# VectorE's work ahead of attention in another order: clears while it waits, the latent's products first, the rotary key's rotation last

## The reference

```
h = rmsnorm(x, g_pre_mix)
q_sb, k_sb, v_sb, q_mla, ckv, k_rope, gate_a, gate_b = jnp.split(h @ w_in, SPLIT_POINTS, axis=-1)
...
q_nope, q_rope = q_mla[..., :MLA_NOPE], rope(q_mla[..., MLA_NOPE:], pos)
ckv = rmsnorm(ckv, ckv_gain)        # the latent, 128 wide
k_rope = rope(k_rope, pos)          # the rotary key: x1*cos - x2*sin, x1*sin + x2*cos
...
o_sb = sb_attend(q_sb, k_sb, v_sb, ...)             # stick-breaking attention, 8 heads of 64
o_lat = mla_attend(q_lat, q_rope, ckv, k_rope, ...) # latent attention
```

## Time and profile before

| | us |
|---|---|
| median of 3 runs | 1912.62 (1909.57 to 1912.67) |
| profiled execution | 1912.68 |
| its span, first to last instruction | 1910.9 |
| TensorE busy | 1853.4 (97%) |
| GpSimd busy | 987.1 (52%) |
| VectorE busy | 964.0 (50%) |
| ScalarE busy | 558.1 (29%) |

### The profile page before, as it was taken

How to read it: one execution, slowest core, us unless ns; L and a number is a source line. 1 busy time by engine, 2 the same in 40 slices (tenths; PEclk the granted TensorE clock), 3 DMA queues, 4 the chain that set the end, 5 groups by cost and what they waited for, 6 DMA issues and landing times. The chain is left out here.

```text
span 1910.9 us, 33493 instructions
## 1 busy us (share of the span) xinstructions
PE 1853.4 (97%) x14390; PEld 1786.2 (93%) x14390; DVE 964.0 (50%) x1536; ACT 558.1 (29%) x1164; POOL 987.1 (52%) x584
## 2 busy tenths in 40 slices
PE   8999999999999999999999899999999999999999
PEld 8888888999999999999998888889999999999998
DVE  6687665322655531524657756653327555225153
ACT  4344443212422221202344344431124222212021
POOL 6454414555455555556554534245555555555553
PEclk9999999999999999999999999999999999999999
DMA  5232211224122222222342212112242222222222
GB/s 173 95 101 67 73 35 49 89 89 147 67 89 89 89 89 89 89 82 86 103 144 85 95 57 72 39 56 92 86 148 73 86 87 88 88 89 89 81 88 92
DMA packets 74804, 168.37 MB, mean 88 GB/s; under 512 B 6112, under 2 KB 33632, under 8 KB 74656
## 3 DMA queue, kind: packets, MB, share of 16 engines
q1 hardware_dynamic: 67328, 158.69, 25.5%
q10 hardware_dynamic: 7328, 7.54, 1.2%
HBM read 156.41 MB, written 9.79 MB: 87 GB/s over the span
## 5 line engine op out<-in xcount | busy, mean ns | idle before, releaser
L1501 PE MATMUL ps<-xn,wsp 128*128 128x272 f32 x7872 | 1013.1, 289 | 21.4 <-issue 13.1
L1501 PEld LDWEIGHTS ps<-xn,wsp 128*128 128x128 f32 x7872 | 993.2, 189 | 27.8 <-issue 16.9
L583 POOL CAST wsp<-raw 128x1024 fp32r<-128x1024 f32 (+2 forms) x278 | 298.4, 1073 | 778.5 <-DMA raw<-in_wstream 626.7
L585 POOL TENSOR_TENSOR wsp<-raw,wsp 128x1024 fp32r<-128x1024 f32 (+2 forms) x278 | 665.3, 2393 | 22.3
L1501 PE MATMUL ps<-R,wsp 128*128 128x272 f32 x3840 | 486.3, 288 | 0.1
L1501 PEld LDWEIGHTS ps<-R,wsp 128*128 128x128 f32 x3840 | 482.7, 189 | 1.3 <-DVE xT L1074 0.5
L1045 DVE SCALAR_TENSOR_TENSOR R<-ps,R 64x256 fp32r<-64x256 f32 (+8 forms) x232 | 127.6, 560 | 72.6 <-ACT R L713 22.7
L1394 DVE TENSOR_TENSOR mix<-ps,rstd 128x272 f32<-128x272 f32 x88 | 38.8, 441 | 202.9 <-PE ps L1501 192.5
L936 ACT ACTIVATE mix<-vv 128x2 f32<-128x2 f32 x88 | 17.9, 204 | 363.0 <-DVE mix L1396 363.0
L1045 DVE SCALAR_TENSOR_TENSOR R<-mix,R 128x544 fp32r<-128x544 f32 (+1 forms) x82 | 74.5, 909 | 80.9 <-ACT R L957 66.9
L1402 DVE SCALAR_TENSOR_TENSOR ps<-mix,vv,ps 128x546 f32<-128x546 f32 x88 | 69.4, 788 | 55.6 <-ACT ps L945 55.6
(11 more groups left out here) (225 smaller groups left out, 1526.8 us busy)
## 6 DMA issues: line engine op xcount, KB each, us to landing
raw<-in_wstream SPq DMA_DIRECT2D x233, 512.0 KB, 3.7
raw<-in_wstream SPq DMA_DIRECT2D x48, 128.0 KB, 2.7
raw<-in_wstream SPq DMA_DIRECT2D x16, 384.0 KB, 3.1
raw<-in_kc SPq DMA_DIRECT2D x8, 512.0 KB, 4.1
raw<-in_vc SPq DMA_DIRECT2D x8, 512.0 KB, 4.2
xT<-in_x_in SPq DMA_DIRECT2D x8, 272.0 KB, 5.1
out_k_out<-mix ACTq DMA_DIRECT2D x8, 272.0 KB, 2.9
xT<-in_x_in SPq DMA_DIRECT2D x1, 2176.0 KB, 8.2
```

The costliest lines, as they stand in the source:

```text
L583: nc.gpsimd.tensor_copy(dst[:, 0, 0:w], part).then_inc(S["w_hi"], 1)
L585: nc.gpsimd.tensor_tensor(dst[:, 1, 0:w], part, dst[:, 0, 0:w].bitcast(F32), ALU.subtract).then_inc(S["w_lo"], 1)
L1501: mm = pe.matmul(z[:, h], w[:, x, (k0 + k) * P:(k0 + k + 1) * P], rhs[:, y, k, h * HT:(h + 1) * HT], start=(k == 0 and (x, y) == (0, 0)), ...
```

## The change

VectorE's list ahead of attention is reordered in both layers, and ScalarE's follows. The two clears come first (in layer 0 ahead of the wait for `roots`, in layer 1 behind the wait for `rstd_done`). Then come the two products with rstd, of the latent and of the rotary key; the four small copies; q's low parts; the latent's normalised product and its low part; k. The rotation of the rotary key and its low part come behind k and ahead of v. ScalarE stores and copies the rotary key behind k's copies. No instruction is added or removed, and TensorE's, GpSimd's and SyncE's lists are the same.

```diff
--- before.py
+++ after.py
@@ -847,11 +847,11 @@
                     rsqrt(("cn", 0), LORA)
                     nc.scalar.preload_act_table_set("sigmoid_and_others")
                     rt_tile()
-                    rope_parts(0)
                     act.wait_ge(S["dve_read"], dread(("cn", 0)))
                     act.dma_start(c_out[layer], craw).then_inc(S["c_st"], 16)
                     ac(cT[:, 0], craw, ACT.Copy).then_inc(S["c_hi"], 1)
                     qk_tile(("k", 0))
+                    rope_parts(0)
                     if layer > 0:
                         act.wait_ge(S["x_st"], 16)
                     else:
@@ -1058,15 +1058,12 @@
                             dve.wait_ge(S["acc_done"], n)
                             v.tensor_tensor(acc[:], acc[:], sq[j % 2], ALU.add).then_inc(S["acc_done"], 1)
 
+                    if layer > 0:
+                        dve.wait_ge(old["rstd_done"], 5)
+                    v.memset(q_smp.bitcast(F32), 0.0).then_inc(S["zeroed"], 1)
+                    v.memset(qr_smp.bitcast(F32), 0.0).then_inc(S["zeroed"], 1)
                     if layer == 0:
                         dve.wait_ge(pre["roots"], 1)
-                    else:
-                        dve.wait_ge(old["rstd_done"], 5)
-                    for a in range(QB):
-                        ins = v.tensor_copy(sq[1][:, DEC * a:DEC * (a + 1)], rstd[:, SEQ:T])
-                    ins.then_inc(S["rt_set"], 1)
-                    v.memset(q_smp.bitcast(F32), 0.0).then_inc(S["zeroed"], 1)
-                    v.memset(qr_smp.bitcast(F32), 0.0).then_inc(S["zeroed"], 1)
 
                     def times_rstd(dst, t):
 
@@ -1107,7 +1104,6 @@
 
                     def rope_rotate(n, t):
                         if n == 0:
-                            times_rstd(halves(rope[0]), t).then_inc(S["dve_read"], 1)
                             dve.wait_ge(S["dve_read"], dread(t))
                             dve.wait_ge(S["trig_in"], 16)
                         else:
@@ -1273,16 +1269,20 @@
 
 
                     times_rstd(halves(craw), ("c", 0)).then_inc(S["dve_read"], 1)
-                    rope_rotate(0, ("kr", 0))
+                    times_rstd(halves(rope[0]), ("kr", 0)).then_inc(S["dve_read"], 1)
+                    for a in range(QB):
+                        ins = v.tensor_copy(sq[1][:, DEC * a:DEC * (a + 1)], rstd[:, SEQ:T])
+                    ins.then_inc(S["rt_set"], 1)
                     qk_tile(("q", 0))
                     dve.wait_ge(S["rstd_done"], 1)
                     dve.wait_ge(S["c_sq"], 1)
                     v.scalar_tensor_tensor(halves(craw), halves(craw), vv[:, V_CG:V_CG + 1], ptile(("cn", 0)),
                                            ALU.mult, ALU.mult).then_inc(S["dve_read"], 1)
-                    rope_low(0)
                     dve.wait_ge(S["c_hi"], 1)
                     lo(cT[:, 1], craw, cT[:, 0], "c_lo")
                     qk_tile(("k", 0))
+                    rope_rotate(0, ("kr", 0))
+                    rope_low(0)
                     if layer > 0:
                         dve.wait_ge(S["x_st"], 16)
                     v_tile(("v", 0))
```

## The result

The change makes the kernel slower: 1922.81 us (median of 6 runs, 1920.41 to 1927.88) against 1911.78 us (6 runs of before, 1909.57 to 1913.07). The ratio is 1.0053, 95% interval 1.0037 to 1.0069. The forecast was 1926.1 with 1916 to 1930. The profiled execution took 1923.15 us with a span of 1921.4, 10.5 us more than before's.

A forecast was written before the change was run, and what follows sets the result against it. TensorE, busy 97% of the span, bounds the kernel, so only its waits count. Layer 0's loss of 1.6, layer 1's 7.6 and the clock's 4.2 add 13.4 us to 1912.68: 1926.1 us, range 1916 to 1930.

The forecast's parts named there:

- the wait of 7 to 8 us: Sign of a right forecast: TensorE waits this long for VectorE's product ahead of v's transposition (L1669) in layer 1.
- The place: Ahead of v's transposition TensorE waited only 0.21 and 0.28 us for VectorE's product of v, which has no slack.
- The gain of 3.54 us in layer 0: Layer 0's head: k starts 1.58 us earlier and v follows k without a wait, at 36.74 instead of 40.28.
- The stalls: v's transposition comes later behind the moved rotation: 1.6 us lost in layer 0, gain included, and 7.6 in layer 1.
- rival 1: Layer 1's low part gets in before GpSimd's subtraction: 5.3 us lost in place of 7.6, total 1923.8; chance 0.25.
- The low part is 0.14 us too late and waits for 999.13: Layer 1: rotary key's low part, ready at 996.88, misses GpSimd's subtraction start at 996.74 and waits for its end.
- the cheap branch: Layer 1: the low part gets in before GpSimd's subtraction, 5.3 us lost; chance 0.25.
- the dear branch: Layer 1: the low part is held by GpSimd's subtraction, 7.6 us lost; the forecast itself, chance 0.42.
- The hold by GpSimd: VectorE operations with two SBUF inputs wait for the running GpSimd operation and end 0.58 us after it.
- The rival of an undisturbed rotation: Rotation runs unheld in both layers: +0.45 us, TensorE waits some 2.5 and 1.9, clock unaffected, 1913.1 us; chance 0.13.
- The clock: TensorE's clock falls to half at each layer's stall ahead of v's transposition, costing 2.1 us each, 4.2 in sum.
- I carry the shift to the end undiminished: Behind v's product attention finds its inputs as before, so the whole +13.4 us reaches the end of the kernel.

The follow-up runs named there:

- the move alone: Kernel before, with only the rotation, low part and high part of the rotary key moved behind k; 1925.21 us, ratio 1.0062.
- its undoing in two ways: Two kernels against the changed one: rotation and its parts moved on behind v's product, 1910.47 us; or back to their places of before, 1909.03 us.
- layer 1 alone: New order in layer 1 only, layer 0 in the order of before; 1921.90 us, ratio 1.0045 to the kernel before.
- the busy wait: Changed kernel plus 36 extra matmuls between step 0's scores and v's transposition, in both layers; 1920.26 us, ratio 1.0048 to before.
- layer 0 alone: New order in layer 0 only, layer 1 in the order of before; 1914.46 us, ratio 1.0009 to the kernel before.

## Why the prediction was right

The mechanism came as I had it in both layers, and the time lies in the range. One term of the sum was too large: the wait of 7 to 8 us that I named as a sign for layer 1 was 5.57.

**The place.** v's product has no slack, and the rotation was put ahead of it: right in both layers, shown by the move alone and by its undoing in two ways.

**The gain of 3.54 us in layer 0.** Measured 3.45 us with the rotation in its old place (q's start to the transposition). The term was right, but the reason for its second half was not the only one: I put 1.96 us of it down to the rotation's leaving the way of the normalised product. The move alone shows that this does take away the wait ahead of v, but it is enough as well that everything in front starts earlier. So the part of the change that costs nothing brings the whole gain by itself.

**The stalls.** Layer 0: 1.6 us forecast, 2.19 - 0.47 = 1.72 measured. Layer 1: 7.6 us forecast; from q's start to the transposition it is 25.94 us instead of 20.64, so 5.3 us. This is rival 1, and here a term of my sum was wrong by 2.3 us. The failed step is "The low part is 0.14 us too late and waits for 999.13". Counted from q's start the low part came 0.16 us earlier than I had it, and GpSimd's subtraction 0.13 us later, so the low part went first. (In the sum itself 995.72 + 1.13 is 996.85, not 996.88, and the cheap branch comes to 5.4.) The two prices are right: in the four traces with the rotation behind k and GpSimd free, the low part came 0.15 and 0.17 us ahead of the subtraction (5.3 us lost in the changed kernel, 5.4 in the move alone) and 0.02 and 0.12 us behind it (7.5 us with layer 1 alone, 7.6 with the busy wait). I gave the dear branch 0.42 and the cheap one 0.25. From one profile of before the two could not be told apart, and the forecast would have been better placed between them, at about 1925.

**The hold by GpSimd.** The rule of counting (ends 0.58 us after GpSimd's operation) matched each held operation. The rival of an undisturbed rotation is excluded by the rows, and its own price was right: with GpSimd held back the waits were 2.31 and 1.88 us against some 2.5 and 1.9 forecast. Its clock was wrong: I let it stay at waits of 2 us, and the rows show 3.1 us lost to it. In the time this is hidden by the spread (1913.1 forecast, 1914.5 measured, 1910 to 1916 by the interval).

**The clock.** 4.2 us forecast. From the transposition's start to the projection's end before took 6.75 us at both places, after 8.47 and 9.38: 1.7 + 2.6 = 4.3 us. Right in sum; the two halves of 2.1 are off by 0.4 and 0.5 in opposite directions, so the sum fits in part by luck.

**The sum.** Measured, the terms are 1.7 + 5.3 + 4.3 = 11.3 us where I had 13.4, and nearly all of that is layer 1's stall. The medians are 11.0 us apart and the spans 10.5. The close fit of 11.3 hides shifts that I left out. At the end of layer 1's head the projection behind the transposition ends at 1012.69 instead of 999.68, 13.0 us later: besides the terms there are the 0.5 us ahead of q in layer 0 and 1.2 us that came up between the two heads. At the end of the span 10.5 are left. So "I carry the shift to the end undiminished" failed too: 1.2 us came up between the two heads, and 2.5 were given back behind the second. Some of what was given back can be seen. In the kernel before, TensorE ran at 1.2 GHz behind the wait of 3.38 us; the rows of before that follow it are
```profile
1083.24 4.99 PE L1637 MATMUL ps<-wsp,R 128*128 128x256 f32 x24
...
1088.91 6.25 PE L1501 MATMUL ps<-xn,wsp 128*128 128x272 f32 x48
```
and those of the changed kernel at the same work
```profile
1094.15 0.62 PE L1575 MATMUL ps<-R 64*128 64x256 f32 x6 [0.99 <-DVE R L1045]
...
1094.80 3.11 PE L1637 MATMUL ps<-wsp,R 128*128 128x256 f32 x24
...
1098.58 6.26 PE L1501 MATMUL ps<-xn,wsp 128*128 128x272 f32 x48
```
The wait was 0.99 us there and the clock stayed up, so the shift went from 12.0 us (1094.15 against 1082.14) to 9.7 (1098.58 against 1088.91). Whether this belongs to the change or to the execution isn't shown. Single executions of the same kernel differ by 4 to 15 us in all, and with GpSimd and the clock in play a shift of phase in attention goes either way. That may also be why layer 0 alone came out 1.5 us under its forecast, though its rows at the head were as expected.

## What to carry to other kernels

Ask of each step that is moved back what stands right behind its new place and how long TensorE can wait for that: here 0.2 us, so even undisturbed a chain of some 5 us (in the kernel in which GpSimd waits, 40.68 to 45.55) could not be hidden, and moving only the cheap part forward was worth 2.6 to 3.0 us. The VectorE operations with two SBUF inputs took their length here from the GpSimd operation beside them (0.72 alone, up to 2.8); where such a chain is critical, count it in GpSimd's steps. Where a forecast hangs on which of two operations comes 0.15 us earlier, give both branches and set the time between them.

## What the runs showed of the hardware that I had not expected

TensorE's clock fell to 1.2 GHz behind waits of only 2.31 and 1.88 us (windows of the kernel in which GpSimd waits: 0.60 in 46 to 48 us and 0.57 in 995 to 997, so it fell at about 46.4 and 995.3, once as work began again and once 0.9 us after), while a wait of 3.27 us behind 36 full-width matmuls left it at 1.0 in every window from 996 to 1004. In the first two cases TensorE had done the eight small matmuls of the scores ahead of the wait and did five transpositions after it; so the length of the wait alone does not decide.

The hold goes both ways and in turn. Behind a held VectorE operation GpSimd's next one is late by what VectorE still needs (1.54 instead of 1.04 us, 2.72 instead of 2.39; 2.78 behind the low part that came first), and then VectorE's next one waits for that. In layer 1's rotation, three operations in a row were held in this way.

It is not only operations with two SBUF inputs. The four small copies, with one SBUF input each, took 1.99 us in layer 0 of the changed kernel, beside GpSimd, and 0.43 in layer 1, where GpSimd stood still (in the kernel before 2.94 and 0.44). The larger clear took 0.91 us in both layers, in layer 0 beside GpSimd's subtraction.
